# First layer of a diffusion trunk on one core: q's quarters swapped by transfers, the bias rows written behind the tiles, the ada chunks in eleven groups

## The chip, the core and the metric

The kernel runs on one core of a Trainium2 chip. TensorE (PE) multiplies matrices, VectorE (DVE), ScalarE (ACT) and GpSimd (POOL) work on elements, and SyncE (SP) issues most of the DMA transfers. ACT can issue transfers too, on a queue of its own. Each engine runs its instructions in order and waits on semaphores for the others. The metric is the time of one execution on the device in microseconds (us); less is better.

## What is computed

Four layers over 256 latent tokens ("x") and 256 context tokens ("z") of width 1024. Layer 0 is differential attention, then come retention, neighbourhood attention and differential attention again; each is followed by a SwiGLU network. The change is in layer 0, and in what runs beside it:

```python
def ada_mod(cond, w, b):
    m = jax.nn.silu(cond) @ w + b                  # w: 1024 x 6144, for c and for c_ctx
    return [a[:, None, :] for a in jnp.split(m, 6, axis=-1)]

x1, x2 = x32[..., : d // 2], x32[..., d // 2:]     # axial_rope, d = 64: halves of 32
return jnp.concatenate([x1 * cos - x2 * sin, x1 * sin + x2 * cos], axis=-1)

s = jnp.einsum('bqnd,bknd->bnqk', q, k) * scale    # _diff_core, 16 half heads
p = jax.nn.softmax(s, axis=-1)
a = p[:, :, 0] - lam * p[:, :, 1]                  # pairs of half heads
return jnp.einsum('bhqk,bkhe->bqhe', a, v)

bias = rpb32[:, dr_idx[:, None, None], dc_idx[None, :, :]]   # layer 2 only
```

## The kernel before

**Tiles.** Activations lie transposed, features on the 128 partitions, tokens along the row (x in columns 0 to 255, z in 256 to 511). Every weight is split into a high and a low part (ACT writes `w_hi`, POOL `w_lo`), and a product takes three matmuls. A "unit" is one weight tile of 128x1024, loaded by SP into a ring of four (`loads`, line 437). The attention of layer 0 has eight tiles t, one for each head of 128 features, that is two half heads. For each tile PE runs the unit of q into bank 6 and that of k into bank 7, the transposes (`turn`, line 808 is their instruction) and the weighted sum of the tile before, and then this tile's scores in the order 0, 1, 2, 4, 5, 3. All other matmuls are recorded on line 616.

**DVE in a tile** (`tile_da` of DVE). First come the weights of the tile before (`weights_`: the reciprocal, then `a_x` and `a_z` on line 2111, which PE's transposes wait for), then the rotation of q and that of k (`rotate`, lines 2061 to 2065), then the maxima of the scores (2083, 2086), between them `subnorm` of the tile before (writes `tmp`, line 2118), and at last `low` (`y_lo`, line 2124). PE's scores wait for `kT`, the score of bank 3 waits for `tmp`. `rotate` works on 32 partitions at a time since the two halves of a half head lie on different partitions: four multiplications of 32x256 write the swapped product to `rot`, a multiplication in the bank and a sum follow.

**ACT in a tile** (`tile_da` of ACT). The exponentials of the tile before (`exps`), `value_rows` (the copy `v_st`, counted by `vst_ready`, and four scalings), the context half of q to `qT` (line 1465), that of k to `kT`, the copies of the transposes, the high parts of two units, then `high` of the tile before: square, rsqrt, the first exponential of this tile, and `y_hi` (line 1436).

**The ada products.** Between these DVE computes the modulation's chunks: one chunk a of `w_ada` (128x1024) times the two conditions, one instruction each on line 1807, two for a chunk. `rest_products(count)` runs the next `count` of 48 (chunks 16 to 39). Where they stand is written out in tables: `ADA_VALUES` before the tiles, `ADA_TILE` for each tile (before the weights, between the rotations, behind them), `ADA_TAIL` around the weights of tile 7, `ADA_PROJECT` in the output projection. SP loads the chunks in the groups of `ADA_GROUPS` (first chunk, semaphore, slots) by `ada_rest_load`. Slots 0 to 19 are buffers of their own; slots 20 to 23 lie in `v_all`, over the values of two tiles each, so a group with slot 23 waits for `vst_ready` of all eight tiles. The first product of a group waits for the whole group.

**The bias rows.** Layer 2 wants its bias in a skewed form, which is written to DRAM once in layer 0: ACT issues one transfer `rpb_skew<-rpb_rows` of 7168 rows of 508 bytes (line 1496), behind tile 1, and SP waits for its end (`skew_out`) before it loads `cond_l` at the start of the feed-forward network.

**Behind the tiles.** PE starts the output projection with tiles 0 to 6 of y, the last transposes and the last weighted sum between, and then waits for `y_lo` of tile 7. DVE has `rest_products(ADA_TAIL[0])`, the weights of tile 7, `rest_products(ADA_TAIL[1])`, and only then `subnorm` and `low` of tile 7.

## Time and profile before

| | |
|---|---|
| median of 3 runs | 2457.72 us (2457.31 to 2457.73) |
| profiled execution | 2459.41 us, its span 2457.6 us |
| PE busy | 2408.2 us, 98% |
| DVE, ACT, POOL busy | 53%, 41%, 45% |
| granted PE clock, mean | 0.994 |
| attention tiles of layer 0 | about 87 to 260 us |

The profile is one execution. Busy time is that of instructions that work on data, not of waits or of issuing transfers. The idle time of an engine that nobody waits for costs nothing. DMA queue q1 holds what SP issues, q10 what ACT issues.

### The profile page before, as it was taken

To read this page: it belongs to the slowest core of one execution; us is meant where nothing else is said; L and a number is where in the kernel's file an instruction comes from. 1 tells how busy PE (TensorE), PEld (TensorE's weight loads), DVE (VectorE), ACT (ScalarE), POOL (GpSimd) and SP (SyncE) were. 2 spreads that over 40 slices of the span, in tenths; PEclk is the share of its full clock that TensorE was granted. 3 is DMA by queue.
4 is the path that set the end of the run, shared out by engine and by line. 5 is a ranking of instruction groups with operands and counts; after the bars stand their busy time and mean duration, and the time that the engine had idled before them with its cause. 6 is when DMAs were issued, how large, how long until landed. Compare 5 with 4: busy or idle time off the path is not lost.

```text
span 2457.6 us, 37377 instructions
## 1 busy us (share of the span) xinstructions
PE 2408.2 (98%) x12338; PEld 1984.1 (81%) x12338; DVE 1307.4 (53%) x2280; ACT 1014.4 (41%) x2032; POOL 1111.9 (45%) x839
## 2 busy tenths in 40 slices
PE   9999999999999999999999999999999999998998
PEld 4666788888888888898888887779888888777998
DVE  8988875657253434356555144656655514474211
ACT  3565443232244334343323244655332324565553
POOL 0432444454444334435445443224544544435996
PEclk9999999999999999999999999999999999999999
DMA  8462445547322222326555333323655532323664
GB/s 341 119 121 85 152 148 197 205 162 231 102 86 83 77 68 85 92 89 215 194 205 189 102 86 91 83 75 96 216 193 205 191 100 94 95 69 95 191 185 129
DMA packets 120869, 340.62 MB, mean 139 GB/s; under 512 B 35537, under 2 KB 41937, under 8 KB 120145
## 3 DMA queue, kind: packets, MB, share of 16 engines
q1 hardware_dynamic: 112754, 333.97, 41.5%
q10 hardware_dynamic: 8032, 5.52, 1.5%
q8 instruction: 55, 0.90, 0.2%
q14 instruction: 28, 0.23, 0.0%
HBM read 334.76 MB, written 4.69 MB: 138 GB/s over the span
## 4 chain that ended last, share of the span: by engine, by line
issue 48%; PE 25%; POOL 22%; DVE 2%; ACT 1%; POOLq 1%; DMA 1%; DVEq 0%; SPq 0%; ACTq 0%
POOL w_lo L609 22%; PE low_banks L616 21%; PE high_banks L616 4%; DVE tmp L1878 1%; DVE h_lo L1886 0%; POOLq L608 0%; POOLq L603 0%; DVE ssum_rstd L1734 0%; DMA xT<-in_xT 0%; DMA ada_raw<-in_ada_w 0%; ACT w_hi L1224 0%; DMA w_raw<-in_weights 0%; ACT lnm L1248 0%; ACT L1640 0%; ACT h_hi L1260 0%
## 5 line engine op out<-in xcount | busy, mean ns | idle before, releaser
L609 POOL TENSOR_TENSOR w_lo<-w_raw,w_hi 128x512 fp32r<-128x512 f32 x832 | 1111.4, 1363 | 1326.8 <-ACT w_hi L1224 1326.0
L616 PE MATMUL low_banks<-h_hi,w_hi 128*128 128x512 f32 (+1 forms) x1792 | 640.8, 358 | 12.0 <-DVE h_lo L1886 8.3
L1224 ACT ACTIVATE w_hi<-w_raw 128x512 fp32r<-128x512 f32 x832 | 473.8, 624 | 398.3 <-PE low_banks L616 192.8
L616 PE MATMUL low_banks<-h_lo,w_hi 128*128 128x512 f32 (+1 forms) x1792 | 633.4, 353 | 0.0
L616 PE MATMUL low_banks<-h_hi,w_lo 128*128 128x512 f32 (+1 forms) x1792 | 633.3, 353 | 0.0
L616 PEld LDWEIGHTS low_banks<-h_hi,w_hi 128*128 128x128 f32 x1792 | 339.4, 189 | 68.2 <-issue 12.1
L1734 DVE SCALAR_TENSOR_TENSOR ssum_rstd<-ada_raw,high_banks 128x1024 f32<-128x1024 f32 x304 | 370.8, 1220 | 42.1 <-DMA ada_raw<-in_ada_w 33.9
L616 PEld LDWEIGHTS low_banks<-h_lo,w_hi 128*128 128x128 f32 x1792 | 339.6, 190 | 46.7 <-issue 1.0
L616 PEld LDWEIGHTS low_banks<-h_hi,w_lo 128*128 128x128 f32 x1792 | 339.5, 189 | 46.1
L1645 ACT ACTIVATE lnm<-low_banks 128x512 f32<-128x512 f32 (+1 forms) x88 | 47.8, 544 | 431.5 <-PE low_banks L616 431.4
L2368 DVE TENSOR_TENSOR tmp<-low_banks,lnm 128x512 f32<-128x512 f32 (+1 forms) x88 | 55.0, 625 | 290.5 <-ACT lnm L1645 286.8
L616 PE MATMUL high_banks<-h_hi,w_hi 128*128 128x512 f32 (+1 forms) x384 | 147.9, 385 | 0.8 <-DVE qT L2065 0.8
L616 PE MATMUL high_banks<-h_lo,w_hi 128*128 128x512 f32 (+1 forms) x384 | 143.1, 373 | 0.0
L616 PE MATMUL high_banks<-h_hi,w_lo 128*128 128x512 f32 (+1 forms) x384 | 143.0, 372 | 0.0
L616 PE MATMUL high_banks<-u_hi,w_hi 128*128 128x256 f32 (+1 forms) x424 | 141.0, 332 | 0.5 <-POOL w_lo L609 0.5
L616 PE MATMUL high_banks<-u_lo,w_hi 128*128 128x256 f32 (+1 forms) x424 | 140.3, 331 | 0.0
L616 PE MATMUL high_banks<-u_hi,w_lo 128*128 128x256 f32 (+1 forms) x424 | 140.3, 331 | 0.0
L616 PE MATMUL low_banks<-u_hi,w_hi 128*128 (+2 forms) x352 | 127.6, 362 | 0.0
L616 PE MATMUL low_banks<-u_lo,w_hi 128*128 (+2 forms) x352 | 127.6, 362 | 0.0
L616 PE MATMUL low_banks<-u_hi,w_lo 128*128 (+2 forms) x352 | 127.6, 362 | 0.0
L1837 DVE SCALAR_TENSOR_TENSOR xT<-high_banks,mod,xT 128x256 f32<-128x256 f32 x52 | 24.6, 480 | 173.8 <-PE high_banks L616 173.6
L2373 DVE TENSOR_TENSOR u_lo<-tmp,u_hi 128x512 f32 (+2 forms) x88 | 65.8, 748 | 60.9 <-ACT u_hi L1650 56.0
(265 smaller groups left out, 3791.1 us busy)
## 6 DMA issues: line engine op xcount, KB each, us to landing
w_raw<-in_weights SPq DMA_DIRECT2D x424, 512.0 KB, 3.7
ada_raw<-in_ada_w SPq DMA_DIRECT2D x152, 512.0 KB, 3.8
ada_first<-in_ada_w SPq DMA_DIRECT2D x24, 512.0 KB, 9.4
v_all<-in_ada_w SPq DMA_DIRECT2D x10, 512.0 KB, 5.5
bias<-rpb_skew SPq DMA_DIRECT2D x64, 64.0 KB, 2.4
rpb_skew<-rpb_rows ACTq DMA_DIRECT2D x1, 3556.0 KB, 32.9
ada_rest<-in_ada_w SPq DMA_DIRECT2D x6, 512.0 KB, 14.4
cond_l<-in_cond SPq DMA_DIRECT2D x3, 1024.0 KB
```

What stands on the lines that cost most here:

```text
L609: nc.gpsimd.tensor_tensor(out=w_lo[:, r, part], in0=w_raw[:, r, part], in1=w_hi[:, r, part], op=ALU.subtract).then_inc(lo_ready, 1)
L616: return nc.tensor.matmul(dst, lhsT, rhs, start=start, stop=stop, **kw)
L1224: nc.scalar.activation(w_hi[:, r, part], w_raw[:, r, part], ACT.Copy).then_inc(hi_ready, 1)
L1645: nc.scalar.activation(lnm[:, 0:L.W], bank[2 * s][:, 0:L.W], ACT.Silu)\
L1734: last = V.scalar_tensor_tensor(out=dump, in0=w, scalar=1.0, in1=cond[:, c, :], op0=ALU.mult, op1=ALU.mult, accum_out=ada_sum[:, r, c:c + 1])
L1837: return V.scalar_tensor_tensor(out=x, in0=src[:, COLS[c]], scalar=gate_of(L, which, m, c), in1=x, op0=ALU.mult, op1=ALU.add)
L1878: V.scalar_tensor_tensor(out=tmp[:, m % 2, COLS[c]], in0=xT[:, m, COLS[c]], scalar=amp[:, L.par, q % 2, m, c:c + 1], in1=rstd[:, COLS[c]], ...
L2368: V.tensor_tensor(out=tmp[:, s, 0:L.W], in0=bank[2 * s + 1][:, 0:L.W], in1=lnm[:, 0:L.W], op=ALU.mult).then_inc(L.u_free, 1)
L2373: V.tensor_tensor(out=row(u_lo, j, L.W), in0=tmp[:, s, 0:L.W], in1=row(u_hi, j, L.W), op=ALU.subtract).then_inc(L.u_lo_ready, 1)
```

## The change

It does four things, all in layer 0.

1. From tile 2 on ACT copies the whole of q (512 columns, scaled) from bank 6 to `qT`, then issues four transfers of 32 partitions x 256 that write the swapped quarters of `qT` to `rot`. DVE's `rotate_swapped` waits for them (`swapped_in`) and takes three instructions of 128x256.
2. The write `rpb_skew<-rpb_rows` is issued behind the loop over the tiles, before the last exponentials, instead of behind tile 1.
3. The products are placed anew: 3 before the tiles, then (0, 0, 1, 0), (0, 0, 1, 1) and six times (1, 3, 0, 1), where the four numbers are before the weights, before the rotation of q, between the rotations and behind them; 10 around the weights of tile 7 as before, 2 in the projection. A product's row in `ada_sum` goes by its chunk alone, so four chunks are summed at a time.
4. The chunks are loaded in eleven groups of mostly two instead of nine of up to six.

Some semaphores that no layer uses are not allocated.

```diff
 ADA_PAIRS = (0, 1, 2, 3, 4, 4, 4, 4)
-ADA_GROUPS = ((16, 0, (16, 17, 0, 4, 1, 5)), (22, 1, (2, 6, 3, 7)), (26, 0, (3,)), (27, 1, (7, 20, 21)),
-              (30, 0, (3, 7)), (32, 1, (20, 21, 22)), (35, 0, (20, 23)), (37, 1, (21, 22)), (39, 0, (20,)))
+ADA_GROUPS = ((16, 0, (16, 17, 0, 1, 5, 2)), (22, 1, (6, 3)), (24, 0, (7, 20)), (26, 1, (21, 3)), (28, 0, (7, 20)),
+              (30, 1, (21, 3)), (32, 0, (22, 20)), (34, 1, (21,)), (35, 0, (22, 23)), (37, 1, (20, 21)), (39, 0, (22,)))
 ADA_MIXER = 40
-ADA_VALUES = 4
-ADA_TILE = ((0, 1, 2), (1, 1, 1), (1, 1, 2), (1, 1, 2), (1, 1, 2), (1, 1, 2), (1, 1, 2), (1, 1, 2))
+ADA_VALUES = 3
+ADA_TILE = ((0, 0, 1, 0), (0, 0, 1, 1), (1, 3, 0, 1), (1, 3, 0, 1), (1, 3, 0, 1), (1, 3, 0, 1), (1, 3, 0, 1), (1, 3, 0, 1))
 ADA_TAIL = (1, 9)
-ADA_PROJECT = (1, 1, 1, 1, 0, 0)
+ADA_PROJECT = (1, 1, 0, 0, 0, 0)
 LOOPED = 4
...
             at = KT + RING
-            load_range(at, 24)
-            sp.wait_ge(ada_done, 25)
+            load_range(at, 22)
+            sp.wait_ge(plan[0].vst_ready, 2)
+            sp.wait_ge(ada_done, 22)
             ada_rest_load(2)
+            load_range(22, 24)
+            sp.wait_ge(plan[0].vst_ready, 4)
+            sp.wait_ge(ada_done, 24)
+            ada_rest_load(3)
+            sp.wait_ge(ada_done, 26)
+            ada_rest_load(4)
             load_range(24, 26)
-            sp.wait_ge(ada_done, 26)
-            sp.wait_ge(plan[0].vst_ready, 4)
-            ada_rest_load(3)
+            sp.wait_ge(ada_done, 28)
+            ada_rest_load(5)
             load_range(26, 28)
-            sp.wait_ge(ada_done, 28)
-            ada_rest_load(4)
+            sp.wait_ge(plan[0].vst_ready, 6)
+            sp.wait_ge(ada_done, 30)
+            ada_rest_load(6)
             load_range(28, 30)
-            sp.wait_ge(ada_done, 30)
-            sp.wait_ge(plan[0].vst_ready, 6)
-            ada_rest_load(5)
+            sp.wait_ge(ada_done, 32)
+            ada_rest_load(7)
             load_range(30, plan[0].nf)
...
-            sp.wait_ge(ada_done, 33)
             sp.wait_ge(plan[0].vst_ready, KT)
-            ada_rest_load(6)
+            sp.wait_ge(ada_done, 34)
+            ada_rest_load(8)
             sp.wait_ge(ada_done, 35)
-            ada_rest_load(7)
-            sp.wait_ge(ada_done, 36)
-            ada_rest_load(8)
+            ada_rest_load(9)
+            sp.wait_ge(ada_done, 37)
+            ada_rest_load(10)
...
                     if L.zq:
+                        a = 0 if place >= 2 else SEQ
                         act.wait_ge(unit_used, t * 2 + (n + 1))
-                        nc.scalar.activation(qT[:, SEQ:TOK], bank[6][:, SEQ:TOK], ACT.Copy, scale=DA_DIM ** -0.5)\
+                        nc.scalar.activation(qT[:, a:TOK], bank[6][:, a:TOK], ACT.Copy, scale=DA_DIM ** -0.5)\
                             .then_inc(L.qk_act, 1)
+                    if L.zq and place >= 2:
+                        act.wait_ge(L.qk_act, t * 2 + 1)
+                        for quarter in range(4):
+                            a, b = 32 * quarter, 32 * (quarter ^ 1)
+                            act.dma_start(rot[a:a + 32, :], qT[b:b + 32, 0:SEQ]).then_inc(L.swapped_in, 16)
                     act.wait_ge(unit_used, t * 2 + (n + 2))
...
                 tile_da(1, n + 2, 0, 1)
+                with own.loop((KT - 2) // 2, 2) as i:
+                    for s in range(2):
+                        tile_da(i * 2 + (2 + s), n + 4 + 2 * s, i, 2)
                 if L.li == 0:
...
                        .then_inc(skew_out, 16)
-                with own.loop((KT - 2) // 2, 2) as i:
-                    for s in range(2):
-                        tile_da(i * 2 + (2 + s), n + 4 + 2 * s, i, 2)
                 exps(KT - 1, range(1, L.banks))
...
                         dve.wait_ge(rest_loaded[s], 16 * loaded)
-                    row = (a - a0) % LOOPED
+                    row = (a - ADA_FIRST) % LOOPED
                     last = V.scalar_tensor_tensor(out=quarters(dump_0[:, :]), in0=ada_slot(slots[a - a0]), scalar=1.0,
...
                         dve.wait_ge(ada_done, a + 1)
-                        if row == LOOPED - 1 or a == a0 + len(slots) - 1:
-                            ada_sums(a - row, a - row, row + 1)
+                        if row == LOOPED - 1:
+                            ada_sums(a - row, a - row, LOOPED)
                 turn[0] += count
...
+            def rotate_swapped(x):
+                V.tensor_tensor(out=rot[:, :], in0=rot[:, :], in1=da_rope[:, 3, :], op=ALU.mult)
+                own(V.tensor_tensor(out=x, in0=x, in1=da_rope[:, 2, :], op=ALU.mult))
+                return V.tensor_tensor(out=x, in0=x, in1=rot[:, :], op=ALU.subtract)
             def attention(L, e0):
...
-                def tile_da(t, place, extra=(0, 0, 0)):
+                def tile_da(t, place, extra=(0, 0, 0, 0)):
                     if place:
...
                         weights_(t - 1)
-                    dve.wait_ge(unit_used, t * 2 + (n + 1))
-                    if L.zq:
-                        dve.wait_ge(L.qk_act, t * 2 + 1)
-                    rotate(bank[6][:, 0:SEQ], qT[:, 0:SEQ], 0).then_inc(L.qk_dve, 1)
                     rest_products(extra[1])
+                    if L.zq and t >= 2:
+                        dve.wait_ge(L.swapped_in, t * 64 - 64)
+                        rotate_swapped(qT[:, 0:SEQ]).then_inc(L.qk_dve, 1)
+                    else:
+                        dve.wait_ge(unit_used, t * 2 + (n + 1))
+                        if L.zq:
+                            dve.wait_ge(L.qk_act, t * 2 + 1)
+                        rotate(bank[6][:, 0:SEQ], qT[:, 0:SEQ], 0).then_inc(L.qk_dve, 1)
+                    rest_products(extra[2])
                     dve.wait_ge(L.qk_act, t * (1 + L.zq) + (1 + L.zq))
...
                     rotate(bank[7][:, 0:SEQ], kT[:, 0:SEQ], 2).then_inc(L.qk_dve, 1)
-                    rest_products(extra[2])
+                    rest_products(extra[3])
                     maxima(t, 0, range(2))
```

On DVE, from behind `a_z` of the tile before to the end of the products behind `kT` (before: tile 5; with the change: tile 5 too; tiles 2 to 7 are alike but for the chunks' slots). Before:

```order
L2061 TENSOR_TENSOR rot<-high_banks,da_rope 32x256 [waits qk_act_0,unit_used]
L2061 TENSOR_TENSOR rot<-high_banks,da_rope 32x256 x3
L2064 TENSOR_TENSOR high_banks<-high_banks,da_rope 128x256 [waits dve_own]
L2065 TENSOR_TENSOR qT<-high_banks,rot 128x256 [waits dve_own]
L1807 SCALAR_TENSOR_TENSOR dump,ada_sum<-ada_first,cond 128x1024
L2061 TENSOR_TENSOR rot<-high_banks,da_rope 32x256 [waits qk_dve_0,qk_act_0,ada_done]
L2061 TENSOR_TENSOR rot<-high_banks,da_rope 32x256 x3
L2064 TENSOR_TENSOR high_banks<-high_banks,da_rope 128x256 [waits dve_own]
L2065 TENSOR_TENSOR kT<-high_banks,rot 128x256 [waits dve_own]
L1807 SCALAR_TENSOR_TENSOR dump,ada_sum<-v_all,cond 128x1024
L1807 SCALAR_TENSOR_TENSOR dump,ada_sum<-v_all,cond 128x1024 [waits dve_own]
L2083 TENSOR_REDUCE d_st<-low_banks 128x1 [waits s_done_0,ada_done]
```

and with the change:

```order
L1826 SCALAR_TENSOR_TENSOR dump,ada_sum<-ada_first,cond 128x1024
L1826 SCALAR_TENSOR_TENSOR dump,ada_sum<-ada_first,cond 128x1024 [waits dve_own]
L1761 TENSOR_TENSOR mod<-ada_sum,bias_ada 128x8 [waits ada_done]
L1826 SCALAR_TENSOR_TENSOR dump,ada_sum<-ada_first,cond 128x1024 [waits rest_loaded0,dve_own]
L2088 TENSOR_TENSOR rot<-rot,da_rope 128x256 [waits swapped_in_0,dve_own]
L2089 TENSOR_TENSOR qT<-qT,da_rope 128x256
L2090 TENSOR_TENSOR qT<-qT,rot 128x256 [waits dve_own]
L2080 TENSOR_TENSOR rot<-high_banks,da_rope 32x256 [waits qk_dve_0,qk_act_0]
L2080 TENSOR_TENSOR rot<-high_banks,da_rope 32x256 x3
L2083 TENSOR_TENSOR high_banks<-high_banks,da_rope 128x256 [waits dve_own]
L2084 TENSOR_TENSOR kT<-high_banks,rot 128x256 [waits dve_own]
L1826 SCALAR_TENSOR_TENSOR dump,ada_sum<-ada_first,cond 128x1024
```

Three products (and a sum that is due at every fourth chunk) now stand between `a_z` and the rotation of q, none between the rotations, and one instead of two behind `kT`; the rotation of q waits for `swapped_in` in place of the bank.

On ACT, behind tile 1 before the change:

```order
L1382 ACTIVATE e_x,d_st<-low_banks,d_st 128x512 [waits negmax_0]
L1436 ACTIVATE y_hi<-tmp 128x512 [waits y_ready_0]
L1496 DMA rpb_skew<-rpb_rows 7168x1x127 [waits skew_in]
L135 UNCONDITIONAL_BRANCH
L135 ISA
L1382 ACTIVATE e_x,d_st<-low_banks,d_st 128x512 [waits negmax_0]
```

and behind the loop over the tiles with it:

```order
L1448 ACTIVATE y_hi<-tmp 128x512
L143 REGISTER_ALU
L143 COMPARE_AND_BRANCH
L1518 DMA rpb_skew<-rpb_rows 7168x1x127 [waits skew_in]
L1394 ACTIVATE e_x,d_st<-low_banks,d_st 128x512 [waits negmax_0] x2
L1400 ACTIVATE e_z,d_st<-high_banks,d_st 128x256 [waits negmax_0]
L1400 ACTIVATE e_z,d_st<-high_banks,d_st 128x256
L1400 ACTIVATE e_z,d_st<-high_banks,d_st 128x256 [waits negmax_0]
L1400 ACTIVATE e_z,d_st<-high_banks,d_st 128x256
L1394 ACTIVATE e_x,d_st<-low_banks,d_st 128x512 [waits negmax_0]
L1408 ACTIVATE v_st<-v_all 128x512 [waits v_dve_0]
```

The write of the bias rows moved from behind `y_hi` of tile 0, in tile 1, to behind `y_hi` of tile 6, in tile 7, ahead of the copy `v_st` of tile 7.

On SP, the loads from the last part of the tiles to the start of the projection's. Before:

```order
L451 DMA v_all<-in_ada_w 128x4x256 [waits vst_ready_0,ada_done]
L451 DMA v_all<-in_ada_w 128x4x256 x2
L437 DMA w_raw<-in_weights 128x1024 [waits lo_ready] x2
L451 DMA v_all<-in_ada_w 128x4x256 [waits vst_ready_0,ada_done]
L451 DMA v_all<-in_ada_w 128x4x256
L451 DMA v_all<-in_ada_w 128x4x256 [waits ada_done]
L451 DMA v_all<-in_ada_w 128x4x256
L451 DMA v_all<-in_ada_w 128x4x256 [waits ada_done]
```

and with the change:

```order
L455 DMA v_all<-in_ada_w 128x4x256
L441 DMA w_raw<-in_weights 128x1024 [waits lo_ready] x2
L455 DMA v_all<-in_ada_w 128x4x256 [waits ada_done]
L441 DMA w_raw<-in_weights 128x1024 [waits lo_ready] x2
L455 DMA v_all<-in_ada_w 128x4x256 [waits ada_done,vst_ready_0]
L455 DMA v_all<-in_ada_w 128x4x256
L455 DMA v_all<-in_ada_w 128x4x256 [waits ada_done]
L455 DMA v_all<-in_ada_w 128x4x256
L455 DMA v_all<-in_ada_w 128x4x256 [waits ada_done]
```

The first group that needs all of `vst_ready` and the two behind it now hold five chunks, 35 to 39, as before; the groups ahead of them are smaller and stand each between two pairs of weight loads.

On DVE behind tile 7, from behind its weights (`a_z`) to `y_lo`, with the change:

```order
L1826 SCALAR_TENSOR_TENSOR dump,ada_sum<-v_all,cond 128x1024
L1826 SCALAR_TENSOR_TENSOR dump,ada_sum<-v_all,cond 128x1024 [waits rest_loaded0,ada_done]
L1826 SCALAR_TENSOR_TENSOR dump,ada_sum<-v_all,cond 128x1024 [waits dve_own]
L1761 TENSOR_TENSOR mod<-ada_sum,bias_ada 128x8 [waits ada_done]
L1826 SCALAR_TENSOR_TENSOR dump,ada_sum<-v_all,cond 128x1024 [waits dve_own] x2
L1826 SCALAR_TENSOR_TENSOR dump,ada_sum<-v_all,cond 128x1024 [waits rest_loaded1,ada_done]
L1826 SCALAR_TENSOR_TENSOR dump,ada_sum<-v_all,cond 128x1024 [waits dve_own]
L1826 SCALAR_TENSOR_TENSOR dump,ada_sum<-v_all,cond 128x1024 [waits ada_done]
L1826 SCALAR_TENSOR_TENSOR dump,ada_sum<-v_all,cond 128x1024 [waits dve_own]
L2143 SCALAR_TENSOR_TENSOR tmp<-high_banks,subln,ssum_rstd 128x512 [waits ors_ready_0,ada_done]
L2149 TENSOR_TENSOR y_lo<-tmp,y_hi 128x512 [waits y_hi_ready_0]
```

The products that wait for `rest_loaded` are the first of chunks 35 and 37; `tmp` and `y_lo` stand behind all nine products, as before, where the first of the nine was the second of chunk 33 and now is the second of chunk 34.


## Rows read from the trace of the kernel before

**Rows 1.** Waits of PE from 86 to 296 us: total us, times, longest.

```profile
PE low_banks L808 <- DVE a_z L2111: 3.1, 2, 1.9
PE low_banks L616 <- DVE kT L2065: 3.1, 2, 2.4
PE low_banks L616 <- DVE tmp L2118: 1.8, 2, 1.1
PE low_banks L616 <- DVE xT L1837: 1.3, 1, 1.3
```

**Rows 2.** Windows: PE, PEld, DVE, ACT, POOL busy (instructions), PEclk, DMA share, GB/s.

```profile
198.00:206.00 8.00, 8.00 (x17) 3.30 (x18) 6.81 (x9) 3.70 (x8) 2.85 (x2) 0.50 0.74 238
```

**Rows 3.** Timeline of PE, 100 to 280 us: start, duration, work [idle before it].

```profile
111.22 1.13 PE L616 MATMUL low_banks<-kT,qT 64*128 64x512 f32 x4 [0.71 <-DVE kT L2065]
...
172.75 1.13 PE L616 MATMUL low_banks<-kT,qT 64*128 64x512 f32 x4
...
197.90 2.08 PE L616 MATMUL low_banks<-kT,qT 64*128 64x512 f32 x4 [2.40 <-DVE kT L2065]
...
243.70 0.70 PE L616 MATMUL low_banks<-kT,qT 64*128 64x512 f32 x2
...
272.00 0.39 PE L616 MATMUL high_banks<-y_hi,w_hi 128*128 128x512 f32 x1
```

**Rows 4.** Timeline of DVE in tiles 3 and 5.

```profile
144.31 0.87 DVE L2111 SCALAR_TENSOR_TENSOR a_z<-e_z,d_st 128x256 f32<-128x256 f32 x2
...
146.97 0.43 DVE L2064 TENSOR_TENSOR high_banks<-high_banks,da_rope 128x256 f32<-128x256 f32 x1
...
151.26 0.42 DVE L2065 TENSOR_TENSOR kT<-high_banks,rot 128x256 f32<-128x256 f32 x1
...
153.40 2.16 DVE L1807 SCALAR_TENSOR_TENSOR dump<-ada_first,cond 128x1024 f32<-128x1024 f32 x1
...
186.52 1.23 DVE L1807 SCALAR_TENSOR_TENSOR dump<-ada_first,cond 128x1024 f32<-128x1024 f32 x1 [4.35 <-DMA v_all<-in_ada_w]
```

**Rows 5.** Timeline of ACT in tiles 3 and 7.

```profile
144.26 0.36 ACT L1465 ACTIVATE qT<-high_banks 128x256 f32<-128x256 f32 x1
...
249.05 0.63 ACT L1436 ACTIVATE y_hi<-tmp 128x512 f32 x1 [0.57 <-DVE tmp L2118]
```

**Rows 6.** The page: DMA issues, KB each, median us from issue to landing.

```profile
v_all<-in_ada_w SPq DMA_DIRECT2D x10, 512.0 KB, 5.5
bias<-rpb_skew SPq DMA_DIRECT2D x64, 64.0 KB, 2.4
rpb_skew<-rpb_rows ACTq DMA_DIRECT2D x1, 3556.0 KB, 32.9
```

**Rows 7.** Line 1496, the bias write: duration in ns and time of its issue.

```profile
L1496 ACTq DMA_DIRECT2D rpb_skew<-rpb_rows x1: 725/725/725, 115.6 to 115.6; - x1
```

**Rows 8.** Line 437 from 133 to 139 us: two weight loads, issue and landing.

```profile
L437 SPq DMA_DIRECT2D w_raw<-in_weights x2: 333/333/333, 134.1 to 137.6; - x2
...
DMA to landing us min/median/max: 10.2/11.2/12.1
```

**Rows 9.** DMA queues from 136 to 140 us (q10 is ACT's): packets, MB, share.

```profile
q10 hardware_dynamic: 855, 0.43, 123.8%
```

**Rows 10.** DMA queues from 142 to 148 us (q1 is SP's).

```profile
q1 hardware_dynamic: 282, 1.02, 63.2%
q10 hardware_dynamic: 262, 0.13, 14.2%
```

**Rows 11.** Timeline of DVE behind tile 7, 258 to 272 us.

```profile
258.26 1.23 DVE L1807 SCALAR_TENSOR_TENSOR dump<-v_all,cond 128x1024 f32<-128x1024 f32 x1
...
259.53 1.23 DVE L1807 SCALAR_TENSOR_TENSOR dump<-v_all,cond 128x1024 f32<-128x1024 f32 x1
...
269.57 0.75 DVE L2118 SCALAR_TENSOR_TENSOR tmp<-high_banks,subln,ssum_rstd 128x512 f32<-128x512 f32 x1 [0.54 <-ACT ssum_rstd L1249]
271.02 0.69 DVE L2124 TENSOR_TENSOR y_lo<-tmp,y_hi 128x512 fp32r<-128x512 f32 x1 [0.70 <-ACT y_hi L1436]
```

More of the change, by code:

```diff
@@ L160, in __init__ @@
         self.first = (5 if self.kind != 1 else 6) if self.zq else KT
-        self.half_done = sem(f"half_done_{li}")
+        if self.zq:
+            self.half_done = sem(f"half_done_{li}")
         self.v_done = sem(f"v_done_{li}")
         self.s_done = sem(f"s_done_{li}")
-        self.osq_ready = sem(f"osq_ready_{li}")
-        self.oms_done = sem(f"oms_done_{li}")
-        self.ors_ready = sem(f"ors_ready_{li}")
+        if self.kind != 2:
+            self.osq_ready = sem(f"osq_ready_{li}")
+            self.oms_done = sem(f"oms_done_{li}")
+            self.ors_ready = sem(f"ors_ready_{li}")
         self.y_ready = sem(f"y_ready_{li}")
@@ L190, in __init__ @@
             self.t_done = sem(f"t_done_{li}")
+            if self.kind == 0 and self.zq:
+                self.swapped_in = sem(f"swapped_in_{li}")
             self.aT_ready = sem(f"aT_ready_{li}")
```

## Prediction

> **What bounds the kernel now.** I read the page first. PE is busy 98% of the span, so time is only there where PE waits, or runs at its lower clock. The list of PE's waits between 86 and 296 us comes next: nearly all of them end with DVE, on its lines for a_z, kT, tmp and xT, together 9.3 us of [rows 1]. So in the first layer's attention DVE sets the pace, though over the whole span it is busy only half of the time. The windows then show what a wait costs beyond itself: after PE had waited 1.2 us for a_z and 2.40 us for kT, it was granted 0.50 of its full clock, the 1.2 GHz level, from 198 to 206 us [rows 2]. Those 8 us did some 4 us of work.
>
> The timeline of PE puts this on a scale. The scores of tiles 1, 4, 5 and 7 start at 111.22, 172.75, 197.90 and 243.70 us [rows 3]. From tile 1 to 4 that is 20.51 us a tile, with no wait that lasts. From 4 to 5 it is 25.15, and from 5 to 7 it is 45.80 for two, so tile 5 and its low clock cost 4.64 + 4.78 = 9.4 us. The cause of tile 5 is on DVE, which stood still 4.35 us for chunks of ada weights that were not loaded yet [rows 4].
>
> **The tiles: what the change gives.** In tile 3 DVE ends a_z at 145.18 and kT at 151.68 [rows 4], 6.5 us: one product of 1.27 (from the start of one to the start of the next, [rows 11]), which leaves 2.6 for each rotation. From tile 2 on, the changed kernel has three products there (3.8), a rotation of q in three instructions of 128x256, and the k rotation (2.6). The bank instruction of the rotation takes 0.43 [rows 4]; three such, a little overlapped, are 1.2. Sum 7.6, so kT comes 1.1 later behind a_z. For that a product behind kT, which takes 2.16 there [rows 4], is gone: the maxima and tmp start about 1 us earlier, until they meet ACT's rsqrt, and I put a_z 0.5 us earlier. The slack of kT before PE's scores shrinks from about 0.6 us to about 0.1, and the tile stays at 20.5 us.
>
> The transfers have to be in by then. ACT copies q at 144.26 [rows 5], now 512 wide: about 0.25 us more, and then it issues four. No row has a transfer of this kind. The nearest is the bias load of 64 KB, 2.4 us to landing [rows 6]; four issues of about 0.4 put the last landing some 3.5 us after a_z, and DVE asks at 3.8. The lower bound is no wait, the upper one, with a chunk's load in front (a v_all chunk takes 5.5, [rows 6]), 2 us in a tile. I take none in most of the six, 0.5 us in all; ACT is idle there, so the issues cost nothing.
>
> At the beginning there is one product less before tile 0 and one less before tile 1's weights, which shortens the chain of DVE by 2.5 us before the 111.22; PE waited for a_z and kT there for 2.65. The chunks now come in smaller groups asked for well ahead: the group that DVE waited for in tile 5 is asked for one tile earlier. I count the 9.4 us in full. Tile 7 loses its wait for tmp, 1.1 us [rows 1], and 0.3 of idle time before it. With the swaps' 0.5 taken off, PE would reach the point where it has nothing left without y_lo of tile 7, which it passes at 272.00 [rows 3], 12.8 us earlier: at 259.2.
>
> **The bias write: what the change costs.** It is 3,556 KB in 508-byte rows and takes 32.9 us [rows 6]. Before, it is issued at 115.6 [rows 7], and nothing that anyone waited for was behind it. Two weight loads are: issued at 134.1 and 137.6, they land after 12.1 and 10.2 us [rows 8]. From 136 to 140 ACT's queue moves 0.43 MB and SP's queue has no line at all [rows 9]; from 142 to 148 SP's moves 1.02 MB and ACT's its last 0.13 [rows 10]. So a load issued behind the write moved nothing until the write was nearly drained, 26.4 us after its issue, and the two had landed 5.8 us later.
>
> In the changed kernel the write stands behind y_hi of tile 6 on ACT. That is issued at 249.05 [rows 5], 5.35 us after the scores of tile 7 began; with the maxima earlier I take 4.7. Scores at 232.3 (243.70 less 2.5 and 9.4, plus 0.5) put the write at 237.0, and the drain at 263.4. Behind it wait the last weight load of SP's pair and the group of chunks 35 and 36, both in v_all, which SP may issue only when v_st of tile 7 is copied. By [rows 8, 10] two loads of 512 KB need 5.8 us after the drain; a third adds 2. The group lands at 271.2.
>
> Who waits for it: the third of DVE's ten products behind tile 7. The product of that place began at 258.26, 14.56 behind the scores; 0.5 less puts it at 246.4, where it now waits for 25 us. Behind it on DVE stand seven more products and then tmp and y_lo of tile 7. Before, the same eight and the tail ran from 258.26 to 271.71 [rows 11]; less 0.54 and 0.29 of waiting in there, and a sum of 0.2 that falls away, that is 12.4 us. y_lo is there at 283.6, and PE, done with all else at 259.2, stands for 24 us. The cover is gone: before, PE passed at 272.00 with 0.3 to spare. It goes on 11.6 us later than before. The later groups are in by then, and the load that waits for the end of the write (cond_l, at 296 before) comes after it.
>
> After such a stand PE will come back at the lower clock. The cost lies between nothing and, by [rows 2] and 2 us beyond, 5 us; the wait is far longer than there, and I take 3.5. Behind the stall the projection has two products fewer between DVE's residuals, so PE's wait of 1.3 for xT [rows 1] goes: -1.5 with what follows. Sum: +11.6 + 3.5 - 1.5 = +13.6 us on the profiled execution's 2459.41, which lies 1.7 above the median of 2457.72. On the median I forecast 2471.
>
> **The rivals.** *The loads share with the write* (chance 0.12). They get half of the engines once both queues have work. Against it speak [rows 9]; for it only that two loads on one occasion are little evidence. The 1.5 MB of three loads need 12 us at half rate from about 239, the group lands at 252, y_lo is there at 264.4, PE stands 5 us and passes 7.6 earlier than before. With 2.5 for the clock and -1.5 behind: 2451. The Trainium skill says this, in "DMA: Bandwidth & Descriptors", section "Queues, rings and completion order": an engine takes turns, packet by packet, between the queues that have work. The trace disagrees from 136 to 140 us.
>
> *The group of chunk 35 is in time* (0.08), if the write is not in front of it or the queue is deeper than I think: -12.8 - 1.5, 2443.
>
> *The swaps come late and the stall stays* (0.10, part of the slower side): 2 us in each of six tiles are +12, then the write and all behind it shift too, 2483.
>
> *The two sides cancel* (0.08): the write drains sooner, or lets one load through and not the others, and the group lands between 253 and 262: 2453 to 2462.
>
> What decides between slower and faster is one number: the landing of the group of chunk 35. Every us of it is a us of the whole, so 13.6 less than the 271.2 that I expect, 257.6, is where the change costs nothing.
>
> **How the numbers follow.** The forecast's case has 0.62, at 2471 and between 2464 and 2478 of its own: 2 us for the issue of the write, 3 for the landing, 2.5 for the clock. Within 0.2% (4.9 us, about what a measurement of this kernel can tell from no change) lie the cancelling case and the edges. Slower: 0.62 + 0.10 = 0.72; faster, the two rivals above and the low edge of the third, 0.21; same 0.07. The range of 2450 to 2480 holds the main case, most of the sharing and the cancelling ones.
>
> **What the profile after would show.** Right: kT's instructions of tiles 2 to 7 end less than 0.5 us before PE's scores; scores of tile 7 near 232; no stall at tile 5 and no window at 0.50 there; DVE idle for some 24 us ahead of a product on v_all, released by its DMA; PE waiting as long for y_lo of tile 7; SP's queue without a byte while ACT's moves the write. Wrong: if the v_all chunks move while the write runs; if DVE waits for the rot transfers in each tile; if PE's clock stays full after the stall.

## The result, and the profile after

The changed kernel takes 2473.38 us (median of 4 runs, 2473.05 to 2473.85) against 2457.72: the ratio is 1.0064, 95% interval 1.0052 to 1.0076. So it is slower, by 15.7 us, and the forecast of 2471 is 2.4 below. The profiled execution has a span of 2471.7 us, 14.1 more than before. In the three later sessions the kernel before took 2457.1, 2457.8 and 2458.2 us (single runs 2455.2 to 2462.1), so a difference of about 1 us between kernels of different sessions says nothing.

PE's waits from 80 to 310 us in the changed kernel (total us, times, longest) answer to [rows 1]:

```profile
PE high_banks L628 <- DVE y_lo L2149: 15.4, 1, 15.4
PE low_banks L628 <- DVE kT L2084: 6.3, 5, 3.1
PE low_banks L820 <- DVE a_z L2136: 0.6, 1, 0.6
PE low_banks L628 <- DVE tmp L2143: 0.2, 1, 0.2
```

One wait of 15.4 us, on y_lo of tile 7, is more than all of [rows 1] together. The one on xT is gone and the one on tmp all but gone, as forecast, and the one on a_z shrank; the one on kT doubled, which was not forecast. The timeline of PE shows where (it answers to [rows 3]; these are the scores of tiles 1, 2, 4, 5, 6 and 7, and the product that needs y_lo):

```profile
108.95 1.81 PE L628 MATMUL low_banks<-kT,qT 64*128 64x512 f32 x4 [2.25 <-DVE kT L2084]
131.43 1.13 PE L628 MATMUL low_banks<-kT,qT 64*128 64x512 f32 x4 [0.28 <-DVE kT L2084]
...
172.98 1.13 PE L628 MATMUL low_banks<-kT,qT 64*128 64x512 f32 x4 [0.35 <-DVE kT L2084]
193.83 1.13 PE L628 MATMUL low_banks<-kT,qT 64*128 64x512 f32 x4 [0.26 <-DVE kT L2084]
217.60 1.24 PE L628 MATMUL low_banks<-kT,qT 64*128 64x512 f32 x4 [3.14 <-DVE kT L2084]
243.13 1.13 PE L628 MATMUL low_banks<-kT,qT 64*128 64x512 f32 x4
...
286.17 0.80 PE L628 MATMUL high_banks<-y_hi,w_hi 128*128 128x512 f32 x1 [15.41 <-DVE y_lo L2149]
```

Tile 1 is 2.3 us ahead of before, tile 4 is 0.2 behind, tile 5 is 4.1 ahead, since the stall for chunks in tile 5 is gone, and tile 7 is only 0.6 ahead. Between 193.83 and 243.13 most of the gain was lost again: 23.8 us from tile 5 to 6 and 25.5 from 6 to 7, where the steps from tile 2 to 5 take 20.6 to 20.9. The windows show where the second loss comes from (PE, PEld, DVE, ACT, POOL busy, PEclk, DMA share, GB/s; they answer to [rows 2]):

```profile
108.00:116.00 8.00, 7.05 (x22) 3.06 (x22) 5.92 (x9) 3.01 (x6) 3.98 (x3) 0.79 0.45 131
219.00:228.00 9.00, 9.00 (x19) 4.77 (x20) 4.38 (x8) 5.88 (x17) 0.00 (x0) 0.50 0.22 63
284.00:288.00 4.00, 1.83 (x4) 1.49 (x5) 1.58 (x3) 0.71 (x2) 0.00 (x0) 0.50 0.60 109
288.00:292.00 4.00, 4.00 (x14) 3.15 (x13) 3.93 (x7) 3.79 (x7) 3.37 (x2) 0.73 0.00 0
```

The granted clock was 0.50, the 1.2 GHz level, from 219 to 228 us, after PE had stood 3.14 us for kT of tile 6. The timeline of DVE has the causes of this loss and of the stall (it answers to [rows 4] and [rows 11]):

```profile
212.62 0.42 DVE L2088 TENSOR_TENSOR rot<-rot,da_rope 128x256 f32<-128x256 f32 x1 [2.29 <-DMA rot<-qT]
...
255.93 1.22 DVE L1826 SCALAR_TENSOR_TENSOR dump<-v_all,cond 128x1024 f32<-128x1024 f32 x1
...
273.64 1.22 DVE L1826 SCALAR_TENSOR_TENSOR dump<-v_all,cond 128x1024 f32<-128x1024 f32 x1 [16.49 <-DMA v_all<-in_ada_w]
...
285.42 0.69 DVE L2149 TENSOR_TENSOR y_lo<-tmp,y_hi 128x512 fp32r<-128x512 f32 x1 [0.70 <-ACT y_hi L1448]
```

In tile 6 DVE waits 2.29 us for the swaps. Behind tile 7 it waits 16.49 us for the chunk whose load stands behind the bias write; from there the seven further products and the tail lead to y_lo. Next come the write's issue and its landing, and the swaps' in tiles 6 and 7 (source lines 1518 and 1485, duration of an issue in ns, then issue to landing in us):

```profile
L1518 ACTq DMA_DIRECT2D rpb_skew<-rpb_rows x1: 672/672/672, 247.8 to 247.8; - x1
...
DMA to landing us min/median/max: 39.1/39.1/39.1
...
L1485 ACTq DMA_DIRECT2D rot<-qT x8: 514/612/614, 206.3 to 236.9; - x8
...
DMA to landing us min/median/max: 1.8/1.9/4.4
```

The queues, in three stretches (packets, MB, share of 16 engines, which passes 100% since packets in flight together are each counted; q10 is ACT's with the write, q1 SP's with the chunks; they answer to [rows 9, 10]). First 253 to 257 us, then 261 to 265, then 265 to 276:

```profile
q10 hardware_dynamic: 915, 0.46, 124.6%
...
q10 hardware_dynamic: 560, 0.28, 76.2%
q1 hardware_dynamic: 211, 0.22, 47.9%
...
q1 hardware_dynamic: 1861, 1.85, 70.3%
q10 hardware_dynamic: 2021, 1.03, 44.0%
```

The loads of chunks 35 and 36 were issued at 253.0 and 253.6. Until 261 SP's queue has no line. From then on both move, packet beside packet, while the write has over half of its bytes still to go; it lands at 287. The weight load issued at 247.6, 0.2 us ahead of the write, landed in 4.2 us: what stood ahead of the write was not held up.

### The profile page after: what moved, and what is told of

It is laid out like the page before. It is cut to its first block, busy times and chain, and to the rows that moved or that the text cites. A ratio compares the mean times of both kernels' runs of the same rounds, so it can differ in the third digit from the quotient of the medians.

```text
span 2471.7 us, 37370 instructions
## 1 busy us (share of the span) xinstructions
PE 2410.8 (98%) x12338; PEld 1985.0 (80%) x12338; DVE 1288.8 (52%) x2258; ACT 1015.5 (41%) x2032; POOL 1105.1 (45%) x839
## 4 chain that ended last, share of the span: by engine, by line
issue 45%; PE 34%; POOL 16%; DVE 2%; ACT 1%; POOLq 1%; DMA 0%; DVEq 0%; ACTq 0%; SPq 0%
PE low_banks L628 29%; POOL w_lo L621 16%; PE high_banks L628 5%; DVE tmp L1897 1%; DVE h_lo L1905 1%; ACT w_hi L1236 0%; POOLq L620 0%; DVE ssum_rstd L1753 0%; POOLq L615 0%; DVE ssum_rstd L1885 0%; DMA ada_raw<-in_ada_w 0%; DVE xT L1856 0%; DMA w_raw<-in_weights 0%; ACT h_hi L1272 0%; ACT lnm L1260 0%
## 6 DMA issues: line engine op xcount, KB each, us to landing
ada_rest<-in_ada_w SPq DMA_DIRECT2D x6, 512.0 KB, 14.2
```

## The experiments

Ratios are against the kernel before, timed beside each. The diffs are excerpts where "..." stands. "Expected" texts call their rival explanations theories, by letters.

**The write alone.** The kernel before, with the write moved behind the loop and nothing else:

```diff
                 tile_da(1, n + 2, 0, 1)
-                if L.li == 0:
-
-                    act.wait_ge(skew_in, 16)
-                    act.dma_start(rpb_skew, rpb_rows[:, :].unsqueeze(1).to_broadcast([7 * NA_HEADS, GRID_W, RPB_PAD]))\
-                       .then_inc(skew_out, 16)
                 with own.loop((KT - 2) // 2, 2) as i:
                     for s in range(2):
                         tile_da(i * 2 + (2 + s), n + 4 + 2 * s, i, 2)
+                if L.li == 0:
+
+                    act.wait_ge(skew_in, 16)
+                    act.dma_start(rpb_skew, rpb_rows[:, :].unsqueeze(1).to_broadcast([7 * NA_HEADS, GRID_W, RPB_PAD]))\
+                       .then_inc(skew_out, 16)
```

> The kernel before, with one thing changed: the bias write is issued behind the loop over the tiles instead of behind tile 1. No swaps, the old groups and tables. Theory A (the late stall comes from the write standing in front of a group of ada weight chunks that DVE needs for a product ahead of y_lo of tile 7): DVE stands some 14 to 17 us for v_all at about 258 us, PE waits as long for y_lo of tile 7, the clock costs 2 to 3 more, and the median is 2473, 14 to 17 above the kernel before. Theory B (the swaps or the smaller groups make the loss, and the write alone is hidden): within 3 us of 2457.7.

2472.72 us, ratio 1.0056 (1.0039 to 1.0073). DVE stands 13.11 us for v_all and PE 12.7 for y_lo:

```profile
PE high_banks L616 <- DVE y_lo L2124: 12.7, 1, 12.7
...
275.91 1.23 DVE L1807 SCALAR_TENSOR_TENSOR dump<-v_all,cond 128x1024 f32<-128x1024 f32 x1 [13.11 <-DMA v_all<-in_ada_w]
```

Theory A holds; the waits are about 1 us under its bounds, the time is as expected. The group is issued at 256.0, 5.3 us behind the write at 250.7, with the old tables and groups. The write's place alone costs as much as the whole change.

**The write back behind tile 1**, all else as changed (the same lines moved the other way).

> The changed kernel, with the bias write issued behind tile 1 as before. The swaps of tile 2 then stand behind the write on ACT's own queue. Theory A1 (what stands behind the write on the same queue moves only when it is drained, some 26 us after its issue): the stall behind tile 7 is gone, but DVE waits for the swaps of tile 2 for 12 to 18 us, PE with it, median 2470 to 2476. Theory A2 (the swaps get through beside the write after a few us): a wait of under 5 us in tile 2, median 2455 to 2461.

2478.61 us, 1.0082 (1.0066 to 1.0099): slower than the change, and 2.6 us above the range that A1 gave. The late stall is gone (y_lo 0.5), and tile 2 has taken it over:

```profile
PE low_banks L628 <- ACT aT L1427: 9.1, 1, 9.1
...
145.38 0.92 DVE L2088 TENSOR_TENSOR rot<-rot,da_rope 128x256 f32<-128x256 f32 x1 [16.14 <-DMA rot<-qT]
...
L1485 ACTq DMA_DIRECT2D rot<-qT x4: 612/612/11545, 125.0 to 137.9; - x4
...
DMA to landing us min/median/max: 7.4/7.8/19.1
```

A2 falls: on its own queue a swap waits until the write is through. The write, issued at 114.6, lands at 144.7, and the four swaps, issued from 125.0 on, at 144.2 to 145.3. The 2.6 us above A1's range have a place too, which I had not expected: one of the four swap issues took 11.5 us, so ACT itself stood, copied aT late, and PE waited 9.1 for that before it waited 5.1 for kT.

**The write in seven parts**, 16 of 64 positions behind tile 1 (that part is not shown) and 8 behind the swaps of each of tiles 2 to 7:

```diff
...
                             act.dma_start(rot[a:a + 32, :], qT[b:b + 32, 0:SEQ]).then_inc(L.swapped_in, 16)
+                        if L.li == 0:
+                            act.dma_start(rpb_skew[:, bass.ds(i * 16 + (16 + 8 * (c - n - 4) // 2), 8), :],
+                                          rpb_rows[:, :].unsqueeze(1).to_broadcast([7 * NA_HEADS, 8, RPB_PAD]))\
+                               .then_inc(skew_out, 16)
...
```

> The changed kernel, with the bias write cut in seven: 16 of the 64 positions behind tile 1, then 8 positions behind the swaps of each of tiles 2 to 7. The same bytes are written in all. Theory A (the one late write is the stall): the wait of 15.4 us for y_lo of tile 7 and the low clock behind it are gone, less 1 to 2 us that come back as waits for xT; each piece of 8 takes an eighth of the 26 us, 3.3 us, and is out of the way before the next swaps; median 2456 to 2459. Rival (any piece, early or late, keeps some load or swap from DVE): waits for v_all or the swaps of 1 to 3 us in several tiles, median 2463 to 2470.

2458.72 us, 1.0002 (0.9992 to 1.0011): theory A.

```profile
PE high_banks L628 <- DVE y_lo L2153: 0.5, 1, 0.5
```

The tile 6 stall is still there (DVE 2.5 us on the swaps, PE 4.4 on kT). A part of 8 positions lands 5.0 to 9.0 us behind its issue, not 3.3, still well before the next tile's swaps.

**The seventh group one product later:**

```diff
             sp.wait_ge(plan[0].vst_ready, 6)
-            sp.wait_ge(ada_done, 30)
+            sp.wait_ge(ada_done, 31)
             ada_rest_load(6)
```

> The changed kernel, where SP asks for the seventh group of ada weights (chunks 32 and 33) one product later, so that its loads are issued behind the four swaps of tile 6 and no longer among them. Theory C (the swaps of tile 6 came 4.4 us late because two loads of 512 KB were issued among them, and the clock fell for that wait): DVE's wait of 2.3 us and the 0.50 window at 219 to 228 us are gone, the scores of tile 7 start near 236 instead of 243, everything behind shifts with them, the stall for y_lo stays at 15 to 16; median 2465 to 2467. Rival D (tile 6 is slow from something else, or the chunk now comes too late for tile 7): no gain, 2472 to 2475.

2467.57 us, 1.0036 (1.0024 to 1.0049): 5.8 less than the change, and 0.6 above the range of theory C, whose other signs are there. Its scores of tiles 6 and 7, and the same stretch's clock:

```profile
216.09 1.13 PE L628 MATMUL low_banks<-kT,qT 64*128 64x512 f32 x4
236.86 1.13 PE L628 MATMUL low_banks<-kT,qT 64*128 64x512 f32 x4
...
219.00:228.00 9.00, 9.00 (x40) 6.32 (x39) 6.67 (x13) 8.13 (x23) 1.74 (x2) 1.00 0.50 138
```

Tile 7 begins at 236.86 instead of 243.13, and no swap of tiles 6 and 7 takes over 1.9 us. PE's stall for y_lo is 16.7.

**Both cures together.**

> The changed kernel with both cures: the bias write in seven parts (16 of 64 positions behind tile 1, 8 behind the swaps of each of tiles 2 to 7) and the seventh group of ada weights asked for one product later, behind the swaps of tile 6. The parts alone gave 2458.7, the later group alone took 5.8 off 2473.4. If the two losses are separate they add up: 2452 to 2454, faster than before by some 0.2%, with neither a wait for y_lo of tile 7 nor a low clock in tile 6. If the piece of the write behind the swaps meets the loads of the group now behind it, DVE waits for v_all in tile 6 or 7 and it stays at 2457 to 2460.

2450.52 us, 0.9965 (0.9952 to 0.9979). They add up, and it is 2 us better than the two alone promised: the two losses are separate. PE's waits for kT are down to 2.8, of which 2.2 are in tile 1.

**Without the swaps:** q is turned by DVE's six instructions in all tiles, with the write whole behind tile 1 and the seventh group at the change's place.

```diff
...
-                    if L.zq and t >= 2:
-                        dve.wait_ge(L.swapped_in, t * 64 - 64)
-                        rotate_swapped(qT[:, 0:SEQ]).then_inc(L.qk_dve, 1)
-                    else:
+                    if True:
...
```

> The changed kernel without the swaps (q of every tile is turned in DVE's six instructions, as in tiles 0 and 1) and with the write behind tile 1: the new tables and groups alone. DVE then needs 1.3 us more ahead of kT in each of six tiles. Theory E (PE waits for kT already at a tile's end by 0.3 us, so every us there is PE's): PE waits 1.0 to 1.6 us for kT in each of six tiles, and the median is 6 to 9 above the kernel with swaps, small parts and the later group, 2459 to 2462. Rival (DVE has room, since it waits 10 us for PE in the maxima): PE's wait for kT stays at 0.3, 2452 to 2455, and the swaps give nothing.

2459.89 us, 1.0010 (1.0001 to 1.0020), 9.4 above the kernel of both cures:

```profile
PE low_banks L626 <- DVE kT L2076: 12.0, 7, 2.2
```

Theory E, with waits a little over its 1.0 to 1.6. PE waits 1.4 to 2.0 us for kT in tiles 2 to 7, though DVE waits 8.0 us for PE in the maxima: what the swaps take off DVE ahead of kT is PE's time. The two kernels differ in the write's and the group's place too, but PE's waits for kT alone are 9.2 us longer here (12.0 against 2.8), and y_lo has a wait of 0.6 in both.

**The products of tiles 0 and 1 moved behind the turn of k**, on top of both cures:

```diff
-ADA_TILE = ((0, 0, 1, 0), (0, 0, 1, 1), (1, 3, 0, 1), (1, 3, 0, 1), (1, 3, 0, 1), (1, 3, 0, 1), (1, 3, 0, 1), (1, 3, 0, 1))
+ADA_TILE = ((0, 0, 0, 1), (0, 0, 0, 2), (1, 3, 0, 1), (1, 3, 0, 1), (1, 3, 0, 1), (1, 3, 0, 1), (1, 3, 0, 1), (1, 3, 0, 1))
```

> The kernel of the two cures, and the one product that tiles 0 and 1 each have between the turn of q and the turn of k moved behind the turn of k. The product took 1.25 us of the 2.25 that PE waits for kT in tile 1, which is followed by a low clock at 108 to 112 us. Theory: 1.2 to 2.5 us less than the kernel of the two cures, 2450 to 2452. Rival (the product only moves in front of the maxima, which then hold up tile 2): no difference between the two.

2446.89 us, 0.9954 (0.9941 to 0.9968): 3.6 less than without, where 1.2 to 2.5 were expected, and all five runs are below all five of the kernel of both cures. Scores of tiles 1 and 7, and the window of the low clock:

```profile
108.33 1.13 PE L628 MATMUL low_banks<-kT,qT 64*128 64x512 f32 x4 [1.18 <-DVE kT L2088]
...
233.41 1.13 PE L628 MATMUL low_banks<-kT,qT 64*128 64x512 f32 x4
...
108.00:112.00 4.00, 3.67 (x14) 1.67 (x16) 3.93 (x6) 1.32 (x2) 4.00 (x3) 1.00 0.45 131
```

The wait fell by 1.07 us, and the clock did not fall behind it, where the profile of both cures has 0.72 from 108 to 120 us. Tile 2's scores follow those of tile 1 by 21.4 us, instead of 24.1; that is the rest. The rival has a small part: PE's wait for kT in tile 2 grew from 0.3 to 0.8. This is the best version found.

That the shorter wait is what kept the clock up is likely, not shown. The same wait of 2.25 us in tile 1 was followed by very different clocks in the kernels of the last write (e11) and of the longer rows (e12) below, which are alike up to there but for the buffer of the bias rows and its filling (windows of e11, then e12):

```profile
108.00:120.00 12.00, 11.12 (x24) 5.30 (x24) 6.69 (x10) 5.88 (x17) 3.92 (x3) 0.57 0.28 87
108.00:120.00 12.00, 10.72 (x41) 6.45 (x42) 9.93 (x18) 7.83 (x22) 4.32 (x3) 1.00 0.29 89
```

In the changed kernel and the one with the later group, which do not differ from the first of these up to there, it was 0.86 and 0.72. Over all profiles with this wait and at most 0.3 in tile 2, the step from tile 1's to tile 2's scores is 20.8 to 25.6 us. What a wait costs in clock is thus a range of nearly 5 us here, and one profile gives one draw from it.

**The write in one piece, later still**, behind the copies of aT of tile 7 (with the later group; the lines go from their place ahead of the last exponentials):

```diff
...
                 turned(KT - 1)
+                if L.li == 0:
+
+                    act.wait_ge(skew_in, 16)
+                    act.dma_start(rpb_skew, rpb_rows[:, :].unsqueeze(1).to_broadcast([7 * NA_HEADS, GRID_W, RPB_PAD]))\
+                       .then_inc(skew_out, 16)
                 high(KT - 1, LAST_O, LAST_MS)
...
```

> The changed kernel with the later group (2467.6), and the bias write in one piece about 9 us later on ACT, behind the copies of aT of tile 7. The loads of chunks 35 to 38 are then issued 7 us ahead of the write, only the load of chunk 39 some 3 us behind it. Theory A (only what is issued behind the write is late, by some 9 us before it moves): chunks 35 to 38 land in about 6 us, DVE waits 4 to 8 us for chunk 39 alone, PE waits 3 to 7 for y_lo, median 2455 to 2461. Rival (the write also slows what was issued ahead of it, or takes the queue whole until it is drained at some 280 us): DVE waits 14 us or more, 2466 to 2472.

2453.29 us, 0.9981 (0.9971 to 0.9990), 14.3 less than with the write ahead of the group, and 1.7 under the lower bound of A. It is issued at 254.8, 7 us after the group it used to delay:

```profile
253.09 1.23 DVE L1826 SCALAR_TENSOR_TENSOR dump<-v_all,cond 128x1024 f32<-128x1024 f32 x1 [1.31 <-DMA v_all<-in_ada_w]
272.76 2.04 DVE L1826 SCALAR_TENSOR_TENSOR dump<-v_all,cond 128x1024 f32<-128x1024 f32 x1 [7.18 <-DMA v_all<-in_ada_w]
```

The chunks issued ahead of the write cost 1.3 us, the one load behind it 7.2. A had PE wait for y_lo, but y_lo does not stand behind that load: it is done at 265.6, and PE waits 2.5 for xT. So what decides is the order of issue.

**Longer rows.** With the later group, and the write in its place behind the tiles, but from four copies of each row (the larger buffer for them is not shown):

```diff
...
-                    act.dma_start(rpb_rows[:, pad:pad + RPB_W], rpb_in).then_inc(skew_in, 16)
+                    act.dma_start(rpb_rows[:, :, pad:pad + RPB_W],
+                                  rpb_in.unsqueeze(1).to_broadcast([7 * NA_HEADS, 4, RPB_W])).then_inc(skew_in, 16)
-                    act.dma_start(rpb_skew, rpb_rows[:, :].unsqueeze(1).to_broadcast([7 * NA_HEADS, GRID_W, RPB_PAD]))
+                    act.dma_start(rpb_skew.rearrange("a (c b) w -> a c (b w)", b=4),
+                                  rpb_rows.rearrange("a b w -> a (b w)").unsqueeze(1).to_broadcast([7 * NA_HEADS, GRID_W // 4, 4 * RPB_PAD]))
...
```

> The changed kernel with the later group (2467.6), the bias write in one piece where the change puts it, behind the tiles, with the same bytes, but read from four copies of each row side by side: 1,792 rows of 2,032 bytes instead of 7,168 of 508. What was measured: 508-byte rows move at 105 to 130 GB/s, 1 KB rows of the weights at up to 390, and SP's queue moved nothing for 8 to 9 us behind the write. Theory G (the write's price goes with its number of rows): it is drained some 10 us behind its issue, the group issued 5.5 us behind it lands in about 8 to 10 us, DVE waits 2 to 7 us for v_all, median 2453 to 2459. Theory H (the price goes with its bytes, or any write in front costs a fixed 13 us): DVE waits over 10 us, median 2462 to 2468.

2461.72 us, 1.0018 (1.0008 to 1.0027). The write lands in 20.0 us instead of 38.5, DVE waits 11.4 instead of 17.0. The queues from 244 to 248 and from 248 to 252 us:

```profile
q10 hardware_dynamic: 452, 0.92, 107.4%
...
q10 hardware_dynamic: 462, 0.94, 91.8%
q1 hardware_dynamic: 123, 0.13, 14.6%
```

The wait and the time are those of theory H (over 10 us; 2462), but neither of its reasons holds as it stands: the bytes are the same, and the wait fell by 5.6 us. Theory G is wrong by more. With a quarter of the rows the write ran at some 230 GB/s, twice as fast, not three times; and the group, issued at 243.5, was without a byte until 250, for over 6 us. Whether it is the number of the rows or their length that sets the write's rate these runs do not tell apart.

**The same, whole and behind tile 1**, on the kernel of 2446.9.

> The kernel of the two cures and the moved products of tiles 0 and 1 (2446.9), but with the bias write whole, in rows of 2,032 bytes, behind tile 1 instead of in seven parts. Theory G: it is drained by 124 us, before the swaps of tile 2 are issued, where the narrow rows held them for 16 us; DVE waits under 1 us for them, and the median is 2445 to 2448, the same as with seven parts. Theory H: the swaps of tile 2 wait 10 us or more, 2457 or above.

2457.93 us, 0.9996 (0.9987 to 1.0005):

```profile
131.20 1.13 DVE L2091 TENSOR_TENSOR rot<-rot,da_rope 128x256 f32<-128x256 f32 x1 [4.73 <-DMA rot<-qT]
```

4.7 us in place of 16.1, so it is the rest of the write that the swaps wait for. But it was not through by 124 us (issued at 114.1, it landed at 130.5), and theory G fails here too; the time is H's (2457 or above), with half of its wait. PE's wait for kT there was 7.1 us. Seven short parts are 11 us better than one faster whole.

## Why the prediction was right, and where its parts were not

The sign, the place and the mechanism were right: the write, moved to where the group of chunks 35 and 36 is issued behind it, makes DVE late for a product ahead of y_lo. The write alone reproduces it (2472.7), its parts remove it. But that the sum was good to 0.5 us in the spans (13.6 against 14.1) is luck: the gain of the tiles was put 11.6 us too high, the stall 9.0 too long and what lies behind it 2.1 too high, and the errors cancel.

**Tiles, -12.8 forecast, -1.2 measured** (PE was out of work at 270.76, which is 286.17 less 15.41, where before it passed at 272.00). Four terms:

- *The 2.5 us at the beginning* are not there. Tile 1 starts 2.3 earlier, but with the low clock now behind its scores (0.79 from 108 to 116 us, 1.7 us of work) and small waits for kT, and by tile 4 PE is where it was. DVE's chain was shortened as forecast, but PE still waits 2.25 us for kT there, and I had costed the wait and not the clock that can follow one. When 1.07 us were taken off it, 3.6 came back.
- *Tile 5, -4.64 forecast, -4.3 measured* (the move from 0.2 behind to 4.1 ahead).
- *Tiles 6 and 7, -4.78 forecast, +3.5 measured* (49.30 us for the two against 45.80). The step that failed is the upper bound of the swaps, "with a chunk's load in front (a v_all chunk takes 5.5, [rows 6]), 2 us in a tile. I take none in most of the six, 0.5 us in all". In tile 6 that case came true: a chunk load was issued at 207.9, ahead of the last swap's 208.2, and a second at 208.5, and that swap landed in 4.4 us instead of 1.9. 2.3 us of DVE became 3.1 of PE and 9 us at half clock (with the write in parts PE waited 4.4 us at this place, and had 0.99 of its clock from 222 to 228). I had priced the case at 2 us, without its clock. With the group one product later these tiles take 41.4 us, 4.5 less than before: the forecast of the tables and the groups was right.
- *Tile 7 to the end of PE's work, -1.4 forecast, -0.7 measured* (27.63 us against 28.30).

**The steady tile.** The forecast had kT 1.1 later behind a_z, a slack of about 0.1 and a tile of 20.5. In tile 3 DVE ends kT 7.7 us behind a_z (7.6 forecast), 0.13 ahead of PE's scores (0.57 before), so this term was right. PE waits 0.26 to 0.35 for kT in tiles 2, 4 and 5, and the tile is 20.6 to 20.9. In tile 4 DVE waits 0.24 for the last swap, which lands at 168.7, 3.8 behind a_z; the issues were sized at 0.4 us each and took 0.61, and two chunk loads went ahead of them. "The issues cost nothing" held: PE's list has no wait for ACT.

**The stall, 24 forecast, 15.4 measured.** The write was issued at 247.8, not 237.0, since the tiles had gained next to nothing, but PE's end of work moved with it. What made the stall shorter is the group: behind the write's issue it took 25.9 us (273.64 less 247.78) where the forecast had 34.2. The step that failed is "a load issued behind the write moved nothing until the write was nearly drained". [Rows 9, 10] show two loads issued at 134.1 and 137.6 that moved at 142, and I took the drain for the cause, since it was at 142 too. In the profile after, loads issued at 253.0 moved from 261, with over half of the write to go: they stand for about 8 us, and then both queues share. The row of before could not tell 8 us from the drain. The write alone shows the same: loads issued at 256.0, and SP's queue moves from 263, with over half of the write to go.

So the rival of sharing was half right, too. The Trainium skill's rule, in "DMA: Bandwidth & Descriptors", section "Queues, rings and completion order", that an engine takes turns between the queues that have work, agrees with 265 to 276 us, where q1 moved 1861 packets and q10 2021. It does not show from 253 to 257, where SP's queue had two loads issued and no line.

**The clock behind the stall, +3.5 forecast, about 2 measured**: 0.9 us of work from 286.2 to 288 at 0.50, and 1.1 from 288 to 292 at 0.73. **xT, -1.5 forecast**: the wait of 1.3 is gone, a new wait of DVE of 1.7 for a chunk hides in PE's slower stretch. PE goes on 14.2 us later than before (-1.2 + 15.4), and the span is 14.1 longer, so what lies behind the stall adds up to nothing, where +2.0 was forecast: +2.0 for the clock, -1.3 for xT, and -0.8 that no row here names.

**Open.** Why SP's queue stands for 6 to 9 us behind the write, before the two share. It is not in proportion to the write's rows: a quarter of them left over 6 us. Nor is it a fixed time: chunk 39's load, issued at 278.9 when the write had under a fifth of its rows left, has its first packet 2 us later. That the last swap of tile 6 was late by the chunk loads is shown by moving those; whether by the engines' work or by their place in a queue is not.

## What to carry to other kernels

Look for each large transfer's neighbours in order of issue, on both queues, up to the next thing that anyone waits for: issuing it 7 us behind a group of loads instead of 5 ahead of it, or cutting it in parts each shorter than the gap to the next small transfer, was worth more than doubling its speed. And cost a wait of TensorE with a range for the low clock that may follow it: here the tiles around the wait of 3.1 were 7.9 longer than without it, while one profile had the full clock behind a wait of 2.25 and another 0.57 over 12 us. Compare medians of several runs, not two profiles. A row in which two things end at the same time does not tell which of them was waited for.

## What was not expected of the hardware

A transfer of 3,556 KB in 508-byte rows left the other queue without a byte for about 8 us, and only then shared packet by packet. Four times longer rows made it twice as fast (20.0 us to landing against 38.5 behind the tiles, 16.4 against 30.1 behind tile 1). Small transfers behind it on its own queue landed up to 19.1 us later, and one of their issues held ACT for 11.5 us. An issue of a 32 KB swap took 0.61 us of ACT, nearly twice that of a weight load on SP (0.33, [rows 8]) and as much as that of a chunk on SP (0.55 to 0.66 in tile 6); one of the chunks issued behind the write held SP for 3.5 us. The same wait of TensorE, 2.25 us in the same tile, came with a mean granted clock from 0.57 to 1.00 between 108 and 120 us.
